# Attention of a two-block model on one Trainium2 core: the row multiply goes from VectorE to ScalarE, and sixteen conv taps change places

## The reference, cut to what matters

```python
zl = hl @ w_in[l] + b_in[l]
q_l, k_l, v_l = qkv_heads(zl, q_gain[l], k_gain[l])          # 8 query heads, 2 key heads, 128 wide
s = einsum('bqhgd,bkhd->bhgqk', qi, k_all) * ATTN_SCALE       # 128 queries x 768 keys at a time
p = softmax(s, axis=-1)
o = einsum('bhgqk,bkhd->bqhgd', p, v_all)
h = depthwise_conv(a * sigmoid(gt), dw_w, dw_b)               # 31 taps over 1024 channels
m = gates[0] * attn_o + gates[1] * conv_o + gates[2] * pool_o
```

## Time and profile before

| | before |
|---|---|
| median of the runs | 3210.1 us |
| the profiled execution | 3205.96 us, span of its instructions 3204.2 us |
| busy, share of the span | TensorE 97%, VectorE 62%, ScalarE 36%, GpSimd 25% |
| mean granted TensorE clock | 0.989 |
| attention of layer 0 | about 384 to 496 us from the span's start |
| context attention | about 496 to 522 us |
| attention of layer 1 | about 1715 to 1837 us |
| gate 2 of layer 1 | about 1895 to 1949 us |

### The profile page before, as it was taken

One profiled execution on the slowest core, in us unless ns is written; L12 is line 12 of the kernel. 1 busy time (PEld: TensorE's weight loads), 2 busy tenths in 40 slices (PEclk: granted clock), 3 DMA queues, 4 the chain that ended last, 5 costly groups with the idle time before them and its releaser, 6 DMA issues.

```text
span 3204.2 us, 43663 instructions
## 1 busy us (share of the span) xinstructions
PE 3095.8 (97%) x16034; PEld 2614.2 (82%) x16034; DVE 1974.9 (62%) x2781; ACT 1142.7 (36%) x1638; POOL 803.8 (25%) x316
## 2 busy tenths in 40 slices
PE   7999999999999999999999998999999999999998
PEld 5889977899989999997787776878886786777776
DVE  4898987744576153457988885663746565255443
ACT  3113354233243121123334535343224436353543
POOL 0001102233323232330021033402444322233312
PEclk8999999999999999999999999999999999999999
DMA  7442101112112111124531022323223211222211
GB/s 281 171 172 79 40 1 47 46 59 105 60 47 66 61 64 66 60 72 148 204 123 39 14 72 73 128 80 98 92 98 108 71 62 53 66 86 73 86 40 66
DMA packets 75307, 270.50 MB, mean 84 GB/s; under 512 B 8592, under 2 KB 9616, under 8 KB 74512
## 3 DMA queue, kind: packets, MB, share of 16 engines
q1 hardware_dynamic: 71376, 256.04, 23.8%
q10 hardware_dynamic: 3776, 12.32, 1.0%
HBM read 263.87 MB, written 4.46 MB: 84 GB/s over the span
## 4 chain that ended last, share of the span: by engine, by line
PE 85%; DVE 8%; ACT 2%; DVEq 2%; issue 1%; DMA 1%; ACTq 0%; SPq 0%
PE ps L616 50%; PE ps L919 11%; PE ps L551 4%; PE ps L732 2%; PE ps L565 2%; PE ps L851 2%; PE ps L1060 1%; PE ps L753 1%; PE ps L720 1%; PE ps L1139 1%; PE ps L665 1%; PE ps L1157 1%; PE ps L874 1%; PE ps L623 1%; DVE x L2167 1%
## 5 line engine op out<-in xcount | busy, mean ns | idle before, releaser
L500 POOL TENSOR_TENSOR w_lo<-w_raw,w_hi 128x1024 fp32r<-128x1024 f32 x312 | 803.6, 2579 | 2367.1 <-ACT w_hi L1261 2367.1
L1261 ACT ACTIVATE w_hi<-w_raw 128x1024 fp32r<-128x1024 f32 x380 | 399.9, 1055 | 577.6 <-PE ps L616 295.5
L616 PE MATMUL ps<-act_hi,w_hi 128*128 128x384 f32 (+1 forms) x2544 | 531.6, 357 | 2.5 <-DVE x L2007 0.7
L616 PE MATMUL ps<-act_lo,w_hi 128*128 128x384 f32 (+1 forms) x2544 | 519.2, 352 | 0.0
L616 PE MATMUL ps<-act_hi,w_lo 128*128 128x384 f32 (+1 forms) x2544 | 518.5, 352 | 0.0
L616 PEld LDWEIGHTS ps<-act_hi,w_hi 128*128 128x128 f32 x2544 | 451.6, 188 | 74.9 <-issue 37.4
L616 PEld LDWEIGHTS ps<-act_lo,w_hi 128*128 128x128 f32 x2544 | 454.3, 188 | 32.3 <-issue 0.5
L616 PEld LDWEIGHTS ps<-act_hi,w_lo 128*128 128x128 f32 x2544 | 454.2, 188 | 32.2
L2007 DVE SCALAR_TENSOR_TENSOR x<-ps,mod,x 128x384 f32<-128x384 f32 (+1 forms) x128 | 64.3, 547 | 282.1 <-PE ps L616 226.4
L2167 DVE SCALAR_TENSOR_TENSOR x<-arena,vec,x 128x512 f32<-128x512 f32 x336 | 235.0, 727 | 0.2 <-issue 0.2
L2159 DVE SCALAR_TENSOR_TENSOR arena<-arena,vec 128x783 f32<-128x783 f32 (+1 forms) x240 | 228.0, 950 | 0.0
(11 more groups left out here) (341 smaller groups left out, 4514.4 us busy)
## 6 DMA issues: line engine op xcount, KB each, us to landing
w_raw<-in_weights SPq DMA_DIRECT2D x380, 512.0 KB, 3.4
arena<-in_ada_w SPq DMA_DIRECT2D x75, 512.0 KB, 4.9
tmp<-in_ada_w SPq DMA_DIRECT2D x21, 512.0 KB, 5.4
x<-in_x SPq DMA_DIRECT2D x2, 1536.0 KB, 19.2
x<-in_x ACTq DMA_DIRECT2D x1, 3072.0 KB, 10.7
arena<-in_pool_w ACTq DMA_DIRECT2D x2, 1024.0 KB, 4.7
x_mid<-x ACTq DMA_DIRECT2D x1, 2048.0 KB, 7.0
x<-x_mid ACTq DMA_DIRECT2D x1, 2048.0 KB, 8.3
```

The lines of the kernel that those rows point to most:

```text
L500: nc.gpsimd.tensor_tensor(WL[:, w], raw, WH[:, w].bitcast(f32), ALU.subtract).then_inc(units_split, 1)
L616: last = nc.tensor.matmul(tile(o, o + b - a), w[:, s * UNIT + k * P:s * UNIT + (k + 1) * P], act[:, k * TOK + a:k * TOK + b], start=(n == ...
L1261: nc.scalar.activation(WH[:, s * UNIT:(s + 1) * UNIT], RAW[:, (s % 2) * UNIT:(s % 2 + 1) * UNIT], ACT.Copy).then_inc(hi_done, 1)
```

## The change

In attention, VectorE keeps the inverse of the row sum and signals it with a new semaphore `_r`; the row multiply becomes an ACTIVATE on ScalarE, `normalized(it + 1)`, placed between the copy of tile `it` and the exponential of tile `it+2`. VectorE's drain between inverse and multiply goes. Before it overwrites an inverse it waits for the multiply two tiles back. This holds for both layers and the context attention, which now shares semaphores with attention (an offset of 32 or 16 in its counts). In layer 1 the taps per tile go from 2, 2 to 2 on even and 3 on odd tiles: 80 in attention, so 16 are left for gate 2, 2 per unit. In layer 0 the taps stay.

```diff
-TAPS_AT = ((13, 7, (3, 3, 4, 4, 4, 4, 4, 4, 2, 0), 4, 1), (9, 7, (2, 2, 3, 3, 3, 3, 3, 2, 1, 0), 2, 2))
+TAPS_AT = ((13, 7, (3, 3, 4, 4, 4, 4, 4, 4, 2, 0), 4, (1, 1)), (9, 7, (2, 2, 3, 3, 3, 3, 3, 2, 1, 0), 2, (2, 3)))
...
+                def normalized(it):
+                    act.wait_ge(*at_least(l, st + "_r", it + 1))
+                    nc.scalar.activation(tmp(it % 2, nk * P), tmp(it % 2, nk * P), ACT.Copy, scale=SMALL[:, 6 + it % 2:7 + it % 2])\
+                        .then_inc(on(l, st + "_p"), 1)
+
                 exponential(0)
                 exponential(1)
+                normalized(0)
                 for it in range(n):
                     copy(it)
+                    if it + 1 < n:
+                        normalized(it + 1)
                     if it + 2 < n:
                         exponential(it + 2)
                     if it % 2 == 1 and it >= 5:
...
-                def normalized(it):
+                def sum_inverted(it):
                     dve.wait_ge(tile_free[it % 2], emptied(l, st, it % 2, it // 2))
-                    V.reciprocal(SMALL[:, 6 + it % 2:7 + it % 2], SMALL[:, 2 + it % 2:3 + it % 2])
-                    dve.drain()
-                    V.tensor_scalar(tmp(it % 2, nk * P), tmp(it % 2, nk * P), SMALL[:, 6 + it % 2:7 + it % 2], None, ALU.mult)\
-                        .then_inc(on(l, st + "_p"), 1)
+                    if it >= 2:
+                        dve.wait_ge(*at_least(l, st + "_p", it - 1))
+                    V.reciprocal(SMALL[:, 6 + it % 2:7 + it % 2], SMALL[:, 2 + it % 2:3 + it % 2]).then_inc(on(l, st + "_r"), 1)
 
                 maximum(0)
                 maximum(1)
                 for it in range(n):
-                    normalized(it)
+                    sum_inverted(it)
                     if it + 2 < n:
                         maximum(it + 2)
                     if also:
-                        also()
+                        also(it)
...
-                    done = conv_taps(l, done, per_tile)
+                    done = conv_taps(l, done, per_tile[it % 2])
```

More of the change, by code:

```diff
@@ L302, in two_blocks @@
             qk_bias=1, h_t=0, h_hi=8, h_lo=8, rope_table=16, norm_sq=10, norm_ms=12, norm_done=12, v_mm=1,
-            glu=8, taps=CH * TAPS, conv_out=8, attn_s=32, attn_max=32, attn_p=32, attn_t=32, attn_o=16,
+            glu=8, taps=CH * TAPS, conv_out=8, attn_s=48, attn_max=48, attn_r=48, attn_p=48, attn_t=48, attn_o=24,
             pool_w=16, q_gated=8, pooled=8, mixed=8, sg_free=20 - 8, merged=8, cact=8, cact_hi=8, cact_lo=8, x_back=16,
@@ L316, in two_blocks @@
                          o_mm=8)
+        behind_attn = dict(attn_ctx_s=32, attn_ctx_max=32, attn_ctx_r=32, attn_ctx_p=32, attn_ctx_t=32, attn_ctx_o=16)
         def on(l, name):
+            name = name.replace("attn_ctx_", "attn_")
             if (l // LAYERS, name) not in named:
@@ L324, in at_least @@
         def at_least(l, name, n):
-            return on(l, name), n + per_layer[name] if l % LAYERS else n
+            return on(l, name), n + per_layer[name] if l % LAYERS else n + behind_attn.get(name, 0)
         def v1(l, name, i=0, n=1):
@@ L2298, in block1, with more_taps @@
                 done = conv_taps(l, done, behind_heads)
-                def more_taps():
+                def more_taps(it):
                     nonlocal done
-                    done = conv_taps(l, done, per_tile)
+                    done = conv_taps(l, done, per_tile[it % 2])
                 dve.wait_ge(tile_free[2], emptied(l, "qkv", 2, KV_HEADS))
```

## The result

The changed kernel takes 3242.67 us (median of five runs, 3239.81 to 3245.27) against 3207.64 us of the kernel before (3206.14 to 3210.15, five runs): 1.0109 times, 95% interval 1.0095 to 1.0123. It is slower by 1.1%, or 35 us; 3239 had been forecast, from a median of 3210.1 before.

A forecast was written before the change was run, and what follows sets the result against it. Attention in layer 1 was held to go by a 6.90 us two-tile loop through VectorE, not by TensorE's 6.60. 3206.0 + 39.2 (attention) - 10.0 (gate 2) = 3235.2, plus 4.1 for the median: 3239, range 3216 to 3253.

The forecast's parts named there:

- The leg of the multiply: In attention, inverse to transposes takes 1.18 us instead of 0.91, with the multiply at 0.92 on ScalarE: 0.27 longer.
- The copy-out behind it: Even tiles: copy-out queued behind ScalarE's multiply starts values 1.43 us behind transposes, not 0.71; 0.72 more in 12 of 15 loops.
- The third tap: Layer 1, odd tiles: VectorE's extra tap lies whole in the critical loop, 0.66 us more per loop.
- Layer 0 and the context attention: Layer 0 12.7 us more, context attention 2.2, and 0.5 for the last tile's multiply behind a copy.
- Layer 1: Its attention: 3 loops of 7.83 us and 12 of 8.55, 22.6 more, plus 0.5 at the end and 0.7 closing sum.
- rival (b): Layer 1 attention: TensorE's clock falls in half of the 15 loops, 1.7 us each, 12 more, 3251; chance 0.13.
- the end of attention: The last tile of a layer has its multiply behind a copy: 0.5 us more each, an estimate.
- the first three loops: Layer 1 attention, loops before the first copy-out: 7.83 us instead of 6.90, 0.93 more each.
- Gate 2: In layer 1, sixteen taps fewer end TensorE's 9.1 us wait, plus 0.9 behind it: gain 10.0 (8.5 to 11.3).
- (a): Attention: copy-out not on the loop, only multiply's leg and third tap count; 20.6 more, less 10.0: 3221 us; chance 0.12.
- (c): Attention: loop falls below TensorE's work, 6.60 us per two tiles in layer 1: 3196 us; chance 0.10.

The follow-up runs named there:

- the taps alone: Kernel before the change with only the taps moved (two on even, three on odd tiles), multiply still on VectorE: 3208.36 us, 1.0008 times.
- the multiply alone: Changed kernel with the taps back at two on every tile and four per unit of gate 2: 3236.02 us, 1.0097 times the kernel before.
- the fastest kernel: Changed kernel with VectorE's inverse of the next tile ahead of maximum and taps, and copy-out ahead of ScalarE's multiply: 3184.48 us, 0.9930 times.

## Why the prediction was right, point by point

The forecast rested on reading attention as a loop and not as busy time, and that held. By its steps:

- **The leg of the multiply.** Forecast 1.18 from inverse to transposes, measured 1.18 (1845.56 to 1846.74), the multiply 0.93 against 0.92.
- **The copy-out behind it.** Forecast values 1.43 behind the transposes, measured 1.43. The next leg, values to scores, is 1.37 in place of 1.30, which I had not seen; so the loops are 8.62 and 7.69, not 8.55 and 7.61. The experiment that moved the copy-out alone gave 25 to 28 us, the largest share of the three causes in this kernel; the shares don't simply add up, since the falls of the clock differ from kernel to kernel.
- **The third tap.** Forecast 0.66 in the loop, measured 0.66 with the taps alone (7.56 - 6.90), and 0.67 with the multiply on ScalarE (7.95 with two taps, 8.62 with three). That its tile matters was confirmed by putting it on the other one.
- **Layer 0 and the context attention.** Forecast 15.4 (12.7, half a microsecond at the end, 2.2), measured 16.8.
- **Layer 1.** Forecast 23.8, measured 30.7. This is the mis-sized term. The loops themselves were right to 0.07. What I had priced as rival (b), with 12 us and a chance of 0.13, came true in part along with the forecast: five loops of 9.85 to 11.52 in place of 8.62, 9.2 us, of which 0.7 is the end of a channel group and 8.5 the clock. Each plain fall cost 1.7 (10.31 - 8.62), as priced. The granted clock was 0.92 over 90 us, between the 1.00 of the forecast and the "below 0.9" of the rival. I had treated the two as alternatives, and they were not. Two smaller terms were off as well: the end of attention took 1.5 more in place of 0.5 (the granted clock was 0.70 from 1875 to 1880), and the first three loops took 0.7 less in place of 2.8 more, since the kernel before had its own falls of the clock there (loops of 8.47 and 8.58 that the sum had taken as 6.90) and the changed kernel had none.
- **What brought the clock down stays open.** In each of the five loops TensorE had stood 1.12 or longer ahead of the transposes, then 0.35 or 0.55 ahead of the values, and the values then ran at the lower level for some of their time. But seven other loops with both pauses (1.12 and 0.55) kept the full clock, and so did the steady loops of the multiply alone (0.46 and 0.55). The kernel in which the pause ahead of the values was taken away kept 1.00 with steady loops of 7.8. That shorter or fewer pauses go with fewer falls is as far as the runs go.
- **Gate 2.** Forecast -10.0, measured -9.7 at the mean and -1.2 right behind it. VectorE is still the last there, by 0.22, so the two are about level.
- **Rivals (a) and (c).** Values 1.43 behind exclude (a) (its terms add up to 20.5 and not 20.6, which moves nothing). For (c), the loop did not fall below TensorE's work, but its condition was the right one: once the inverse is not held back by the taps, attention goes at 6.48 to 6.63. I had put TensorE's own work at 6.60 from one interval of 3.30; it is 6.48.
- **Luck.** That 3239 lies within 4 us of the measured time is in part luck. The forecast was a rise of 29.2; the profiled executions rose by 33.8 and the medians by 35.0. The 4.1 us by which I had put the median above the profiled execution came from three runs; over five it is 1.7. And nearly 3 us fell away in stages that the change doesn't touch.

## What to carry to other kernels

Between engines with queues in order, cost an operation that moves by what stands behind it in its new queue and by who waits for that, and not by the idle share of the engine. Write the loop down leg by leg from one timeline; if the legs add up to the measured interval, each edit can be added to it by hand; here that was right to 0.1 us in 7 to 9. Look also at what such a sum takes as constant, here the clock. And before moving work to make room, see whether the small result that everybody waits for (here one inverse of 0.16 us) can be put ahead of the long work in the queue it is in.

## What the runs showed of the hardware

- TensorE's granted clock fell in five of twelve loops that had two pauses, of 1.12 and 0.55 us with the transposes, 0.87, between them (two of the five had a longer first pause, 2.33 and 1.85). In such a loop of 8.62 us at full clock TensorE was busy for 6.94. With pauses of 0.46 and 0.55 in loops of 7.96 it stayed at 1.00, and so it did with one pause of 1.12 in loops of 7.82. A plain loop hit by it took 10.3 in place of 8.62.
- A float32 ACTIVATE of 768 columns in place, with one scale per row, took 0.93 us; VectorE's multiply of the same took 0.62.
- After the start of values that follow a copy-out, the next group started 1.37 later (1839.55 to 1840.92), and 1.30 later where there was no wait (1768.23 to 1769.53 in the fastest kernel).
